# Memory heads in a pipeline, token loads in SP's queue, and sums told tile by tile in a two-block model kernel

## What is computed

```python
h = modulate(x, norm_g, shift, scale)        # shift, scale, gate: rows of silu(c) @ ada_w + ada_b
y_ctx, y_lat = mixer_ab(h_ctx, h_lat, ...)   # layer 0: gated heads and memory heads
x = x + gate1 * rmsnorm(y_lat, norm_g)
x = x + gate2 * rmsnorm(swiglu(modulate(x, ...), w_in, w_out), norm_g)
...
y = moe_experts(h) + sigmoid(h @ w_sg) * shared(h)   # second block
x = x + gt2 * rmsnorm_2(y, norm_w)
```

## Time and profile before

| What | Value |
|---|---|
| Time, median of 3 runs | 2932.03 us (2928.23 to 2935.8) |
| Time of the profiled execution | 2935.02 us |
| Its span, first to last instruction | 2933.2 us |
| Mean granted TensorE clock | 0.939 of full speed |
| PE, DVE, ACT, POOL busy | 85%, 29%, 15%, 7% of the span |
| DMA | 722 MB, 246 GB/s over the span |

### The profile page before, as it was taken

How to read it: one execution, slowest core, us unless ns; L and a number is a source line. 1 busy time by engine, 2 the same in 40 slices (tenths; PEclk the granted TensorE clock), 3 DMA queues, 4 the chain that set the end, 5 groups by cost and what they waited for, 6 DMA issues and landing times.

```text
span 2933.2 us, 33956 instructions
## 1 busy us (share of the span) xinstructions
PE 2494.8 (85%) x13698; PEld 1342.9 (46%) x13698; DVE 844.3 (29%) x1770; ACT 436.3 (15%) x810; POOL 203.1 (7%) x267
## 2 busy tenths in 40 slices
PE   5998996799999998899989877767699988777676
PEld 3454555444444445444476433333277854323222
DVE  3155638510120036400033311111157652111011
ACT  1032221110010012200010100000123421000001
POOL 3122111110010011010010100000000020000000
PEclk8999998899999999999999998888889989989888
DMA  6676578244445353144663799999941357999997
GB/s 247 213 240 249 204 253 301 94 165 157 144 165 171 129 168 122 68 161 151 219 193 128 309 414 415 415 421 416 363 134 55 92 207 305 412 408 419 421 407 292
DMA packets 265449, 722.16 MB, mean 246 GB/s; under 512 B 15312, under 2 KB 149104, under 8 KB 211952
## 3 DMA queue, kind: packets, MB, share of 16 engines
q1 hardware_dynamic: 251808, 690.00, 62.2%
q0 software_dynamic: 13520, 30.41, 3.1%
HBM read 719.17 MB, written 1.18 MB: 246 GB/s over the span
## 4 chain that ended last, share of the span: by engine, by line
PE 68%; DMA 19%; DVE 7%; SPq 2%; ACT 2%; issue 2%; POOL 0%; DVEq 0%; ACTq 0%; POOLq 0%
PE ps L914 24%; DMA ring<-in_moe_w_up 16%; PE ps L1530 10%; PE ps L1027 8%; PE ps L939 5%; PE ps L1129 4%; PE ps L1111 3%; SPq L561 2%; PE ps L1083 2%; PE ps L1647 2%; PE ps L950 1%; PE ps L919 1%; DMA ring<-in_ada_w 1%; PE ps L1303 1%; PE ps L1518 1%
## 5 line engine op out<-in xcount | busy, mean ns | idle before, releaser
L914 PE MATMUL ps<-ring,hT 128*128 128x512 f32 x1632 | 724.9, 598 | 17.7 <-ACT hT L1774 12.2
L914 PEld LDWEIGHTS ps<-ring,hT 128*128 128x128 f32 x1632 | 308.5, 192 | 385.3 <-issue 366.9
L1530 PE MATMUL ps<-arena 128*32 128x512 f32 x1536 | 283.9, 716 | 153.4 <-DMA ring<-in_moe_w_up 149.5
L1530 PE MATMUL ps<-ring,arena 128*32 128x512 f32 x512 | 283.1, 716 | 0.0
L1027 PE MATMUL ps<-ring,arena 128*128 128x512 f32 x528 | 232.2, 592 | 2.4 <-ACT arena L1855 2.4
L1530 PEld LDWEIGHTS ps<-arena 128*32 128x32 f32 x1536 | 72.2, 127 | 338.9 <-issue 235.4
L2361 DVE SCALAR_TENSOR_TENSOR arena<-ps,arena 128x256 f32<-128x256 f32 x66 | 28.0, 425 | 578.9 <-ACT arena L1851 578.7
L939 PE MATMUL ps<-hT,ring 128*128 128x256 f32 x768 | 174.7, 390 | 2.5 <-ACT hT L1774 1.5
L939 PEld LDWEIGHTS ps<-hT,ring 128*128 128x128 f32 x768 | 150.0, 197 | 25.0 <-ACT hT L1774 2.3
L1027 PEld LDWEIGHTS ps<-ring,arena 128*128 128x128 f32 x528 | 100.1, 190 | 127.7 <-issue 127.7
L1553 PE MATMUL ps<-ring,arena 128*32 128x512 f32 x1024 | 131.3, 658 | 22.1 <-ACT arena L2146 21.3
(11 more groups left out here) (543 smaller groups left out, 2434.8 us busy)
## 6 DMA issues: line engine op xcount, KB each, us to landing
ring<-in_moe_w_down SPq DMA_DIRECT2D x128, 1024.0 KB, 17.0
ring<-in_ada_w SPq DMA_DIRECT2D x48, 2048.0 KB, 12.5
arena<-in_moe_w_gate SPq DMA_DIRECT2D x96, 1024.0 KB, 11.3
arena<-in_moe_w_up SPq DMA_DIRECT2D x96, 1024.0 KB, 9.7
ring<-in_ffn_w_in SPq DMA_DIRECT2D x66, 1024.0 KB, 8.8
ring<-in_ffn_w_out SPq DMA_DIRECT2D x33, 1024.0 KB, 5.0
ring<-in_moe_w_gate SPq DMA_DIRECT2D x32, 1024.0 KB, 15.6
ring<-in_moe_w_up SPq DMA_DIRECT2D x32, 1024.0 KB, 17.6
```

The source lines that it names most:

```text
L914: m = pe.matmul(o3, lhsT_of(k), ring[:, a:a + 2, k * EH:(k + 1) * EH], start=start and k == 0, stop=stop and k == KC - 1)
L1530: m = pe.matmul(ps[a * CAP:(a + 1) * CAP, 6, :].rearrange("p (u c) -> p u c", u=2), x_slots[:, k, a * CAP:(a + 1) * CAP], slot_pair(gate_s ...
```

## The change

- SP loads the context tokens behind the third group and the latents behind the fourth. Each pair has a semaphore of its own. PE takes the four groups each followed by its rows and its spread. DVE reads the rows of three groups, squares the context tiles, reads the fourth group's rows, squares the latent tiles, makes the context's scale and two tiles, and then the latents' scale and two tiles.
- `p_sb` exists twice, one for each direction. ACT makes the gap (`Relu` with a negated column as bias) as well as the exponential, on the columns that see a key. The scores of blocks 2 and 3 share bank 2, and the groups use bank 3. DVE makes the weights of turn i + 1 (`weighted`) ahead of reading turn i, with one product for the four triangles. PE makes the row maximum of turn i + 2 and the next head's scores ahead of turn i's output. On DVE the rows of the groups are read behind the wait for `out_g` and behind the sums of squares.
- The last feed-forward of layer 1 tells the first tile's sums ahead of the second's. In the experts' stages the scatter tells each tile (`tile_0_scattered`, `tile_1_scattered`), the product of zeros goes, and the down loads wait for `tile_0_scattered`, told by the second of the four scatter products.
- Some semaphores take the place of others with the same order.

```diff
-        p_sb = A(4, NT)
+        p_at = A.at
+        p_sb = A(2, 4, NT)
...
             return ps[:, FILL_BANK[f], :]
+        def own_blocks(b):
+            at = p_at + b * 4 * NT
+            return arena[:, at:at + 4 * (NT + P)].rearrange("p (s n) -> p s n", s=4)[:, :, 0:P]
+        def seen_by(si, d):
+            return slice(si * P, NT) if d == 0 else slice(0 if si < 2 else SEQ, NT if si < 2 else (si + 1) * P)
+        def scores_of(si, cols):
+            return ps[:, si, cols] if si < 2 else ps[:, 2, slice(cols.start - SEQ * (3 - si), cols.stop - SEQ * (3 - si))]
         def ada_group_of(g):
...
-                used_gate_up, used_down = sem("quad_gate_up_used"), sem("quad_down_used")
+                used_gate_up, used_down = sem("quad_gate_up_used"), sem("tile_0_scattered")
...
                 for s in range(SLOTS):
-                    free_at[s] = n.block if s in DOWN_SLOT else 0
-
-            ada_groups(FIRST_GROUPS)
+                    free_at[s] = 0
+            def tokens(i, src):
+                sp.dma_start(x_sb[:, 2 * i:2 * i + 2, :], src.rearrange("(t p) d -> p t d", p=P)).then_inc(tokens_loaded[i], 16)
+            ada_groups(FIRST_GROUPS - 1)
+            tokens(0, I["ctx"][0])
+            ada_groups(1)
+            tokens(1, I["x"][0])
...
             for j in range(12):
+                if j == DOWN_SLOT[0]:
+                    sp.wait_ge(sem("tile_0_scattered"), QUADS)
...
                 group_bias(g)
-            for i, src in enumerate((I["ctx"][0], I["x"][0])):
-                load(x_sb[:, 2 * i:2 * i + 2, :], src.rearrange("(t p) d -> p t d", p=P), x_loaded)
...
                                               start=first and j == 0, stop=False, skip_group_check=True)
+                        if tile_told and t == 0:
+                            m.then_inc(sem("first_sums_complete"), 1)
                     m.then_inc(block_done, 1)
...
-            for g in range(2):
+            for g in range(4):
                 ada_groups(1, FIRST_BANK[g])
-            pe.wait_ge(constants_loaded, 48)
-            for g in range(4):
-                if g < 2:
-                    ada_groups(1, FIRST_BANK[g + 2])
+                if g == 0:
+                    pe.wait_ge(constants_loaded, 48)
...
-            for hd in range(MLSTM_HEADS):
+            def head_scores(hd):
                 q0 = 64 * (hd % 2)
                 qh, kh = qk[q0:q0 + 64, hd // 2, :], qk[q0:q0 + 64, 2 + hd // 2, :]
-                if hd >= 1:
-                    pe.wait_ge(sem("ml_weights"), 8 * hd)
                 for si in range(4):
                     c0 = 0 if si < 2 else SEQ
-                    m = pe.matmul(ps[:, si, c0:NT], kh[:, si * P:(si + 1) * P], qh[:, c0:NT], start=True, stop=True)
+                    m = pe.matmul(scores_of(si, slice(c0, NT)), kh[:, si * P:(si + 1) * P], qh[:, c0:NT], start=True, stop=True)
                 m.then_inc(sem("ml_scores"), 1)
+            def row_max(i):
+                row = 32 * (i % 2) + i // 2
+                pe.matmul(ps[:, 4 + i % 2, :], ident[0:ROWS, row:row + 1].broadcast_to([ROWS, P]), rows_d,
+                          start=True, stop=True).then_inc(sem("ml_max"), 1)
+            row_max(0)
+            row_max(1)
+            head_scores(0)
+            pe.wait_ge(tp_evacuated, n.tp)
+            for hd in range(MLSTM_HEADS):
                 for d in range(2):
                     i = 2 * hd + d
                     pe.wait_ge(sem("ada_rows_ready"), ada_next[0])
-                    if i >= 2:
-                        pe.wait_ge(sem("ml_weights"), 4 * (i - 1))
-                    row = 32 * d + hd
-                    pe.matmul(ps[:, 4 + d, :], ident[0:ROWS, row:row + 1].broadcast_to([ROWS, P]), rows_d,
-                              start=True, stop=True).then_inc(sem("ml_max"), 1)
-                    ada_groups(ADA_B[i], 5 - d)
+                    ada_groups(ADA_B[i], 3)
                     if i == 0:
                         pe.wait_ge(sem("ml_v_ready"), 4)
-                    pe.wait_ge(sem("ml_weights"), 4 * (i + 1))
-                    pe.wait_ge(tp_evacuated, n.tp)
+                    pe.wait_ge(sem("ml_weights"), i + 1)
+                    if i + 2 < 2 * MLSTM_HEADS:
+                        row_max(i + 2)
+                    if d == 1 and hd + 1 < MLSTM_HEADS:
+                        head_scores(hd + 1)
                     if i >= 1:
                         pe.wait_ge(sem("ml_out_read"), i)
                     for ti in range(4):
...
-                                          p_sb[:, si, ti * P:(ti + 1) * P], v_tok[:, si, hd, :],
+                                          p_sb[:, d, si, ti * P:(ti + 1) * P], v_tok[:, si, hd, :],
...
-                            if last and t == 0 and half == 0:
-                                m.then_inc(S("quad_down_used"), 1)
+                        if last:
+                            m.then_inc(S(f"tile_{t}_scattered"), 1)
...
-                pe.matmul(ps[:, 3, :], zero_t[:, 0:P], zero_t[:, :], start=False, stop=True, skip_group_check=True) \
-                    .then_inc(block_done, 1)
-                n.block += 1
...
                 nc.scalar.preload_act_table(ACT.Sqrt)
                 for i in range(2):
-                    update_tile(i, complete)
+                    wait_for_sums(i)
+                    update_tile(i, None)
+            def feed_forward_sums(i):
+                act.wait_ge(block_done, n.block) if i == 1 else act.wait_ge(sem("first_sums_complete"), 1)
+            def both_updated_and_normed(wait_for_sums):
+                both_updated(wait_for_sums)
                 for i, t in enumerate(LAT):
                     act.wait_ge(x_updated, n.x - 1 + i)
                     tell(nc.scalar.activation(junk[:, :], x_sb[:, t, :], ACT.Square, scale=float(D) ** -0.5,
...
-            act.wait_ge(sem("mean_square"), 1)
-            tell(nc.scalar.activation(stat[:, 1, 0:4], stat[:, 0, 0:4], ACT.Sqrt, scale=1.0 / D, bias=eps_t[:, :]), sem("rms_ready"))
+            nc.scalar.preload_act_table(ACT.Sqrt)
             act.wait_ge(sem("vectors_spread"), 2)
             nc.scalar.copy(v_shift[:, :], spread_view(0, 1)).then_inc(sem("spread_read"), 1)
             nc.scalar.copy(lat_shift, spread_view(0, 0)).then_inc(sem("spread_read"), 1)
-            n.normed = 1
+            for i in range(2):
+                act.wait_ge(sem("mean_square"), i + 1)
+                tell(nc.scalar.activation(stat[:, 1, 2 * i:2 * i + 2], stat[:, 0, 2 * i:2 * i + 2], ACT.Sqrt, scale=1.0 / D, bias=eps_t[:, :]),
+                     sem("rms_ready"))
+            n.normed = 2
             for t in range(4):
...
+                act.wait_ge(sem("ml_max"), i + 1)
+                if i >= 2:
+                    act.wait_ge(sem("ml_out"), i - 1)
                 for si in range(4):
-                    k = 4 * i + si
-                    act.wait_ge(sem("ml_gap"), k + 1)
-                    w = p_sb[:, si, (0 if si < 2 else SEQ):NT]
-                    tell(nc.scalar.activation(w, w, ACT.Exp, scale=-1.0), sem("ml_exp"))
+                    nc.scalar.activation(p_sb[:, d, si, seen_by(si, d)], ps[:, 4 + d, seen_by(si, d)], ACT.Relu,
+                                         bias=colsT[:, 0, si, row:row + 1]).then_inc(sem("ml_gap"), 1)
+                for si in range(4):
+                    act.wait_ge(sem("ml_gap"), 4 * i + si + 1)
+                    w = p_sb[:, d, si, seen_by(si, d)]
+                    nc.scalar.activation(w, w, ACT.Exp, scale=-1.0).then_inc(sem("ml_exp"), 1)
...
-            dve.wait_ge(x_loaded, 32)
-            for t in range(4):
-                do(V.tensor_tensor_reduce(out=h[:, 0, :], in0=x_sb[:, t, :], in1=x_sb[:, t, :], scale=1.0,
-                                          scalar=0.0, op0=ALU.mult, op1=ALU.add, accum_out=stat[:, 0, t:t + 1]))
-            tell(V.tensor_copy(note[:, :], eps_t[0:1, :]), sem("mean_square"))
-            dve.wait_ge(sem("rms_ready"), 1)
-            do(V.reciprocal(stat[:, 2, 0:4], stat[:, 1, 0:4]))
-            n.normed = 1
-            for g in range(4):
+            def squared(i):
+                dve.wait_ge(tokens_loaded[i], 16)
+                for t in (2 * i, 2 * i + 1):
+                    do(V.tensor_tensor_reduce(out=h[:, 0, :], in0=x_sb[:, t, :], in1=x_sb[:, t, :], scale=1.0,
+                                              scalar=0.0, op0=ALU.mult, op1=ALU.add, accum_out=stat[:, 0, t:t + 1]))
+                tell(V.tensor_copy(note[:, :], eps_t[0:1, :]), sem("mean_square"))
+            def first_scale(r, dst):
+                dve.wait_ge(sem("rms_ready"), 2 - r)
+                do(V.reciprocal(stat[:, 2, 2 - 2 * r:4 - 2 * r], stat[:, 1, 2 - 2 * r:4 - 2 * r]))
+                do(V.scalar_tensor_tensor(out=dst, in0=spread_view(1, r), scalar=1.0, in1=v_tmp[:, :], op0=ALU.add, op1=ALU.mult))
+            for g in range(3):
                 ada_rows(1, FIRST_BANK[g])
+            squared(0)
+            ada_rows(1, FIRST_BANK[3])
```

(36 more changed lines are left out.)

48 lines of the change are left out of this document (26 added, 22 removed).

## The result

The changed kernel takes 2902.41 us (median of 4 runs, 2902.09 to 2904.9) against 2932.99 for the kernel before beside it (4 runs, 2928.23 to 2935.8): a ratio of 0.9899, interval 0.9882 to 0.9916, 30.6 us faster. The forecast was 2893.0 with 2882 to 2908; the sum had 39.2 us.

The account below looks back on a forecast made before the run. The prediction read PE as 68% of the path, DMA 19%, DVE 7%. Opening 8.2, heads 23 and closings 8.0 sum to 39.2 us, from 2935.0 to 2895.8 profiled, against the median 2893; range 2882 to 2908.

Parts of the forecast that it names:

- Opening, 8.2: Start of the kernel: reordered token loads and one scale ahead bring the first block to 42.8, 8.2 us saved.
- the stages follow from one another, so this is kept: Behind the opening: the 8.2 us won at the first block stay won through the later stages.
- Rival B: Opening: the first block waits for its weights, 2 us saved instead of 8.2, 2899 us; chance 0.10.
- Heads, 23: Memory heads: the last read ends at 512 instead of 535.2, 23 us saved, bounds 10 and 30.
- The biases hold turns 2 to 4 at 12 us each: Memory heads: biases of groups 6, 8 and 10, behind POOL's stores, hold these turns, turn 4's rows until 482.5.
- just inside the 12: Memory heads: groups' weights come at 5.7 us each, 11.4 per turn of two, within the turn's 12 us.
- Rival A: Memory heads: PE sets the pace, last read ends at 525, 10 us saved instead of 23, 2906 us; chance 0.16.
- Rival C: Memory heads: ACT changes tables between maximum and exponential, two 1.28 us loads per turn, 2901 us; chance 0.06.
- Closings, 8.0: Closings: 2.6 us in each of two experts' stages and 2.75 in layer 1's feed-forward, bounds 5 and 8.5.
- Down loads, 0: Experts' rounds: down loads issued 0.9 us later cost nothing, as 13 us of work are in the queue.
- rival D: Experts' rounds: later down loads cost 3.1 us in each of 30 rounds, 93 in all, 2986 us; chance 0.04.
- E: Heads and opening: stores and loads set both, only the closings' 8 us are left, 2924 us; chance 0.03.

Follow-up runs that it names:

- opening_alone: The kernel before with only the opening's part of the change; 2932.14 us, 0.9988 of the kernel before.
- after: First profile of the changed kernel, set against the kernel before; 2902.41 us, ratio 0.9899.
- after_again: The changed kernel unaltered, run and profiled a second time on another chip's comparison with the kernel before; 2899.74 us, 0.9883.
- down_late: The changed kernel with the down loads waiting for the second tile's scatter products instead of the first's; 2898.47 us, 0.9884 of the kernel before.
- pe_later_3: The changed kernel with three more passes of 16 matmuls in the feed-forward ahead of the attention stage; 2918.8 us (one run).
- pe_later_1: The changed kernel with one more pass of 16 matmuls in the feed-forward ahead of the attention stage; 2914.53 us (one run).

## Why the forecast was right, and where its terms were off

The time lies in the range, 9.4 us above the point. The kinds of gain were those foreseen; some of their sizes were off, and in part they were off in opposite ways. By the prediction's own steps:

**Opening, 8.2: too much.** The fourth group landed at 31.50, not 30.5, and the latents' squares began behind its rows, at 34.5, not 33.5. "Then one scale: 6.55" came out as 6.56 (37.58 to 44.14). So 6.9 were saved at the first block, and its own 9.87 against 9.29 left 6.3, still there at 240 us. The step that failed is "the stages follow from one another, so this is kept": ahead of the heads 3.5 were left in this profile and 4.7 in `opening_alone`, though 7.2 and 7.3 in others with the same opening, and `opening_alone` has 3.4 at the end of its span. The loss is time at the lower clock. In the profile of the change 2.7 us of it went in one block of sixteen products, before (first) and after; over 376 to 388 us the granted clock was 1.00 before and 0.72 after:

```profile
384.83 7.13 PE L1129 MATMUL ps<-ring,hT 128*128 128x512 f32 x16 [2.75 <-DMA ring<-in_ab_w_in]
378.67 9.86 PE L1150 MATMUL ps<-ring,hT 128*128 128x512 f32 x16 [2.62 <-DMA ring<-in_ab_w_in]
```

All fourteen profiles agree with this. The stretch from the last transposed block (L1111 before) to the last product of L1193 has the same work in all of them. It takes 152.1 to 152.5 us in seven, at a mean granted clock of 0.96, 153.7 to 154.4 in four, at 0.94, and 155.4 to 155.7 in three, at 0.93. The kernel before is one of the seven and the profile of the change one of the three (windows of that stretch, before and after):

```profile
240.07:392.58 152.51, 133.41 (x1448) 73.25 (x1447) 88.83 (x176) 37.42 (x52) 21.59 (x38) 0.96 0.66 233
233.75:389.15 155.40, 136.42 (x1448) 74.42 (x1447) 88.84 (x176) 37.40 (x52) 21.95 (x38) 0.93 0.65 232
```

Why the clock falls in one execution and not in another stays open. Rival B is out: the weights did not hold the block.

**Heads, 23: right in size, 21.6 and 21.2 at the place, but by other steps, and in part by luck.** The wait of the rows for the gain vector, foreseen, came: 9.45 us. The first read was at 441.97 and the second at 450.39, before the 453 to 455 of the forecast, since turn 1 took 8.4 us and not 12. "The biases hold turns 2 to 4 at 12 us each" failed. POOL's chain ran back to back as forecast, the eight stores from 439.45 to 480.89 at 5.9 us a link, but DVE waited only 1.9 us for biases in all. What held those turns was the groups' weights ("just inside the 12", as the prediction had it): turns of 8.4, 9.1 and then 19.8, as PE stood for a group and then worked at the lower clock. From there DVE set the pace, as said, though at 7.1 us a turn rather than 8.2. The last read ended at 510.3 against the 512 forecast because these errors cancel in this execution, which is luck. The changed kernel's program up to the end of the heads ran in five profiles (`after`, `after_again`, `down_late`, `pe_later_3`, `pe_later_1`). From the last product of L1193 to the last output they take 113.9 to 119.8 us, where the kernel before takes 139.4. That is 19.6 to 25.5 us saved, and the 23 lies among them. The output projection did not wait for its weights: its first block, at 518.50, waited 0.73 for ACT alone. Rival A gave 525 for the end of the last read and is out as a whole, though its mechanism is what turn 3 shows for one turn.

**ACT's part.** Maximum and exponential take 1.78 and 1.56 us for four blocks (fewer columns than before), and a table load stands between them once, in turn 0 at 424.95; the next is at 497.23, behind the last turn, for the root. Rival C is out. The move to ACT cost the path nothing: DVE waits for the exponential once, 5.87 us ahead of turn 0's weights (427.01), where its wait of 9.45 us for the gain vector follows, and not in the seven turns behind it. The maximum takes ACT 1.78 us for 1280 columns, 1.39 ns each; before, it took DVE 2.19 for 1536, 1.43 ns each. The rule of the Trainium skill ("ScalarE: Activation LUTs", Rules for kernel authors), relu and max on VectorE, gives its factor of about 3 for bf16. In float32 the traces here show no such factor.

**Closings, 8.0: right** at their places: 2.58 in the first experts' stage, 2.5 at the end (last scatter 27.6 earlier, the span 30.1) and 2.7 at the feed-forward. There it is 13.3 us from the last down product to the next block, where it was 16.0. The second tile's reciprocal is at 1451.30, that is the tile's end, 1449.66, plus the 1.55 of the step and 0.1. The three together are 7.8; the time alone gives 7 and can't say it more closely than 2.3 to 11.5.

**Down loads, 0: right,** and `down_late` shows that a longer wait costs nothing either: rival D is out. So is E: the heads gave 19 us alone.

**What the sum did not have** is the clock: the attention's 3.5, and the 2.9 that the stretch ahead of the heads took longer. With the opening's 3.5 instead of 8.2, the heads' 21.6 instead of 23, and 3.5 given back, 39.2 becomes 29.6, against 30.6 measured. These are the terms of one pair of executions. With `after_again` in the place of `after` the opening keeps 7.2, the heads bring 25.5, and the spans differ by 35.2, though its median, 2899.74, is only 2.7 us below the first.

No version here is shown to beat the changed kernel: those with the early vector have 0.9861 to 0.9885, the changed kernel 0.9883 and 0.9899, with intervals that overlap. Their last output starts between 3.8 us earlier and 1.2 later than in `after_again` (499.25), and 6.4 to 11.4 earlier than in the first profile of the change.
